# Pool and dense layer of a two-layer trunk: norm rows spread by products, first units in plain fp32, the dense norm put off, and dense steps of 512 columns

## The reference, cut to what matters

```python
for i in range(DEPTH):
    h = rms_norm(x, norm_g[i, 0])
    y = pool_mixer(h, ...) if i == 0 else forgetting_attention(h, ...)
    x = x + rms_norm(y, norm_g[i, 1])
    h = rms_norm(x, norm_g[i, 2])
    y = swiglu(h, ...) if i == 0 else moe_swiglu(h, ...)
    x = x + rms_norm(y, norm_g[i, 3])
```

## Time and profile before

| | |
|---|---|
| median of three runs | 1280.48 us (1279.67 to 1280.71) |
| the profiled execution | 1283.84 us, of which the span is 1281.9 us |
| PE busy | 1224.0 us (95%) |
| DVE, ACT busy | 698.7 us, 542.9 us |
| bytes read | 412.52 MB, 323 GB/s over the span |
| start of the dense layer's second gate unit | 56.69 us |
| end of the dense layer on PE | 238.45 us |
| start of the first pair of heads | 278.58 us |
| last product of the attention's output | 381.24 us |

### The profile page before, as it was taken

One profiled execution on the slowest core, in us unless ns is written; L12 is line 12 of the kernel. 1 busy time (PEld: TensorE's weight loads), 2 busy tenths in 40 slices (PEclk: granted clock), 3 DMA queues, 4 the chain that ended last, 5 costly groups with the idle time before them and its releaser, 6 DMA issues.

```text
span 1281.9 us, 17304 instructions
## 1 busy us (share of the span) xinstructions
PE 1224.0 (95%) x6616; PEld 886.0 (69%) x6616; DVE 698.7 (55%) x781; ACT 542.9 (42%) x516; POOL 105.3 (8%) x119
## 2 busy tenths in 40 slices
PE   8899999889999999999899999989999989999996
PEld 8799999778878788633588853468883347888332
DVE  5754544656657889400598920078871026887102
ACT  4434343355535677300577710067760025775001
POOL 0000000000001222010005001000501000050100
PEclk9899999999999999999999999999999998999999
DMA  9955656453336899999999999999999999999995
GB/s 301 321 195 168 195 166 195 127 165 104 129 120 235 326 373 366 337 401 402 409 409 404 407 409 409 402 409 409 402 409 409 403 407 409 409 402 381 399 402 216
DMA packets 151065, 414.67 MB, mean 323 GB/s; under 512 B 8704, under 2 KB 48640, under 8 KB 150912
## 3 DMA queue, kind: packets, MB, share of 16 engines
q1 hardware_dynamic: 150032, 409.79, 84.6%
q0 software_dynamic: 960, 3.80, 0.9%
HBM read 412.52 MB, written 1.05 MB: 323 GB/s over the span
## 4 chain that ended last, share of the span: by engine, by line
PE 85%; DMA 5%; DVE 4%; issue 2%; SPq 2%; ACT 2%; DVEq 0%; ACTq 0%
PE bank L1229 20%; PE bank L1230 19%; PE bank L1231 19%; PE bank L1516 14%; DMA raw<-in_moe_w_gate 4%; PE bank L1529 4%; SPq L473 1%; PE bank L1469 1%; PE bank L1592 1%; DVE raw_lo L789 1%; PE bank L1546 1%; ACT w_hi L532 1%; DMA raw<-in_pool_w 1%; PE bank L1236 1%; PE bank L1414 1%
## 5 line engine op out<-in xcount | busy, mean ns | idle before, releaser
L789 DVE TENSOR_TENSOR raw_lo<-raw,w_hi 128x2048 fp32r<-128x2048 f32 x170 | 388.4, 2299 | 142.8 <-ACT w_hi L532 142.6
L532 ACT ACTIVATE w_hi<-raw 128x2048 fp32r<-128x2048 f32 x170 | 325.2, 1916 | 225.2 <-PE bank L1231 160.3
L1229 PE MATMUL bank<-w_hi,h_hi 128*128 128x512 f32 (+1 forms) x848 | 301.6, 356 | 30.8 <-DVE h_lo L1084 10.2
L1231 PE MATMUL bank<-w_hi,h_lo 128*128 128x512 f32 (+1 forms) x848 | 296.8, 350 | 0.0
L1230 PE MATMUL bank<-raw_lo,h_hi 128*128 128x512 f32 (+1 forms) x784 | 272.1, 347 | 0.0
L1229 PEld LDWEIGHTS bank<-w_hi,h_hi 128*128 128x128 f32 x848 | 165.0, 195 | 59.9 <-DVE raw_lo L789 22.6
L1231 PEld LDWEIGHTS bank<-w_hi,h_lo 128*128 128x128 f32 x848 | 165.1, 195 | 20.4
L1230 PEld LDWEIGHTS bank<-raw_lo,h_hi 128*128 128x128 f32 x784 | 153.0, 195 | 16.7
L1516 PE MATMUL bank<-raw,h_b 128*64 128x512 f32 (+1 forms) x768 | 143.3, 523 | 0.8 <-DMA raw<-in_moe_w_up 0.7
L1229 PE MATMUL bank<-w_hi,aT_hi 128*128 128x512 f32 x312 | 123.9, 397 | 1.5 <-DVE aT_lo L925 1.5
L1231 PE MATMUL bank<-w_hi,aT_lo 128*128 128x512 f32 x312 | 121.7, 390 | 0.0
(11 more groups left out here) (240 smaller groups left out, 1283.7 us busy)
## 6 DMA issues: line engine op xcount, KB each, us to landing
raw<-in_moe_w_gate SPq DMA_DIRECT2D x96, 1024.0 KB, 15.9
raw<-in_moe_w_up SPq DMA_DIRECT2D x80, 1024.0 KB, 16.1
raw<-in_moe_w_down SPq DMA_DIRECT2D x64, 1024.0 KB, 14.3
raw_extra<-in_moe_w_down SPq DMA_DIRECT2D x48, 1024.0 KB, 16.2
raw_extra<-in_moe_w_up SPq DMA_DIRECT2D x32, 1024.0 KB, 13.5
raw_extra<-in_moe_w_gate SPq DMA_DIRECT2D x16, 1024.0 KB, 14.2
raw<-in_ffn_w_gate SPq DMA_DIRECT2D x11, 1024.0 KB, 5.4
raw<-in_ffn_w_up SPq DMA_DIRECT2D x11, 1024.0 KB, 5.3
```

Source lines behind the costliest of these rows:

```text
L532: nc.scalar.activation(w_hi[:, slot, :], raw_slot(source), ACT.Copy).then_inc(hi_ready, 1)
L789: nc.vector.tensor_tensor(lo_slot(source), raw_slot(source), w_hi[:, slot, :].bitcast(f32), ALU.subtract).then_inc(lo_ready, 1)
L1229: mm(out, a_hi, b_hi, start=first, stop=False)
L1231: return mm(out, a_lo, b_hi, start=False, stop=last)
```

## The change

It touches four places.

First joint. SP loads the three rows (first pre norm, pool scale, first post norm) as single rows of 4 KB, and PE spreads each over the partitions with two products of a row of ones (`row_spread`); DVE's first norm reads its row from PSUM, ACT copies the others to `scale` and `gain`. The pool's product and the first gate and up units (256 columns) take raw weights and a single unsplit activation `h_whole` in plain fp32 (`ffn_first`), so units 0 to 2 are not split. The dense layer's pre norm is put off: x itself is transposed, the channel gain (`gain_t`, loaded as 1024 single floats) is put in as `h_whole` is written, and the token's factor `rstd` goes into the silu and into the product with up. The filler products are 14 instead of 24 at the start, two new lots of 8, and 16 instead of 32 before the transposes.

Dense layer. After the first 256 columns there are five steps of 512: two gate units, two up units and two down units, with the two token blocks in banks of their own, and six slots for the rounded part instead of three. In the last step token block 0 is finished first, and the next joint's transposes for it stand inside the last down unit.

Second joint. `scale_bank(3, 1)` and its chain come after token block 0's `h_lo`. The forget gate's product is made for each token block (128 columns) instead of once for both (256). `head_row` is loaded once `V_U0 + 2` is used.

Third joint. Three parts of the output product, (0, 0), (1, 0) and (0, 1), come ahead of the last heads' transposes.

```diff
-WARM_START = 24
-WARM = (32, 30, 10, 8, 28, 8)
+WARM_START = 14
+WARM = (16, 6, 10, 8, 28, 8, 8, 8)
...
+            for i, row in enumerate((norm_g[0, 0:1, :], pool_scale, norm_g[0, 1:2, :])):
+                sp.dma_start(norm_row[0:1, i, :], row).then_inc(rows_in, 16)
             sp.dma_start(bands[:, :, :], bands_d).then_inc(bands_in, 16)
             load(0, pool_w[0].rearrange("g (b p) n -> p (g b) n", p=P), FG)
-            sp.dma_start(scale[:, :], pool_scale.to_broadcast([P, D])).then_inc(scale_in, 16)
-            sp.dma_start(gain[:, 1, :], norm_g[0, 1:2, :].to_broadcast([P, D])).then_inc(gain_first[1], 16)
             sp.dma_start(consts[:, :], consts_d).then_inc(consts_in, 16)
+            sp.dma_start(gain_t[:, :], norm_g[0, 2, :].rearrange("(k p) -> p k", p=P),
+                         allow_slow_non_contiguous=True).then_inc(gain_t_in, 16)
...
-            hi(0)
-            input_hi(0)
+            row_copy(1, scale, bank[2:4])
+            row_copy(2, gain[:, 1, :], bank[6:8])
+            for b in (0, 2):
+                sc.wait_ge(tr_done, b + 1)
+                nc.scalar.activation(input_part(h_whole, 0, b), bank_blocks(0, b), ACT.Copy).then_inc(whole_act, 1)
             post_squares(1, 0, in_y, (y_done, 2), in_v)
-            hi(1)
+            sc.wait_ge(gain_t_in, 16)
+            whole_act_part(0)
+            post_squares(1, 1, in_y, (y_done, 4), in_v)
             squares(2, 0)
-            post_squares(1, 1, in_y, (y_done, 4), in_v)
-            hi(2)
-            input_hi(1, [0])
+            dense_hi(0)
+            hi(WHOLE_UNITS)
+            whole_act_part(1)
+            dense_hi(1)
             squares(2, 1)
-            input_hi(1, [1])
+            hi(WHOLE_UNITS + 1)
...
+            for s in range(LAST_FS):
+                g = u_gate(s + 1)
+                hi_upto(g + 4)
+                aT_high_dense(s, 0)
+                hi_upto(g + 5)
+                if s > 0:
+                    aT_high_dense(s, 1)
+                for tb in range(TB):
+                    silu_dense(s + 1, tb)
+                hi_upto(g + 7)
...
+            def norm_first(tb):
+                for half in range(2):
+                    cols = slice(half * HALF, (half + 1) * HALF)
+                    nc.vector.scalar_tensor_tensor(xn[:, tb, cols], x[:, tb, cols], rstd[:, 0, tb:tb + 1],
+                                                   bank[4 + half][:, :], ALU.mult, ALU.mult).then_inc(xn_half, 1)
+            def whole_dve_part(tb):
+                ve.wait_ge(tr_done, 4 + 2 * tb + 2)
+                for k in range(4):
+                    step = nc.vector.tensor_scalar(h_whole[:, 4 + k, tb * P:(tb + 1) * P],
+                                                   bank[2 * tb + 1][:, k * P:(k + 1) * P], gain_t[:, 4 + k:5 + k], None,
+                                                   ALU.mult)
+                step.then_inc(whole_dve, 1)
...
-            scale_bank(3, 1, y, ffn_out, None, False)
             root(4, 0)
             norm_x(4, 0)
+            input_lo(2, [0])
+            scale_bank(3, 1, y, ffn_out, (unit_used, V_U0), True)
             root(3, 1)
-            input_lo(2, [0])
             scaled_ready()
             add_normed(3, 1, y)
...
+            def row_spread(i, banks):
+                for half in range(2):
+                    step = mm(banks[half][:, :], silu[0:1, 0:P], norm_row[0:1, i, half * HALF:(half + 1) * HALF],
+                              start=True, stop=True)
+                step.then_inc(rows_psum, 1)
...
+            pe.wait_ge(rows_in, 48)
+            row_spread(0, bank[4:6])
+            row_spread(1, bank[2:4])
+            row_spread(2, bank[6:8])
+            keep_warm(WARM[6], ones)
             pe.wait_ge(bands_in, 16)
-            pe.wait_ge(xn_done, 1)
...
+            pe.wait_ge(rows_done, 2)
+            for k in range(KB):
+                if k % 4 == 0:
+                    pe.wait_ge(xn_half, k // 4 + 1)
                 pool_first(k)
-            pe.wait_ge(xn_done, 2)
-            for k in range(0, KB, 2):
-                pool_second(k)
-                pool_first(k + 1)
-                pool_second(k + 1).then_inc(tr_done, 1)
-            hi, lo = weights(0, FG)
+            pe.wait_ge(rows_done, 4)
+            keep_warm(WARM[7], ones, bank[7])
+            for k in range(KB):
+                if k % 4 == 0:
+                    pe.wait_ge(xn_half, 2 + k // 4 + 1)
+                step = pool_second(k)
+                if k % 2 == 1:
+                    step.then_inc(tr_done, 1)
...
-                        step = three(to, h_hi[:, k, tok], h_lo[:, k, tok], hi[:, k, :], lo[:, k, :], i == 0, i == 1)
+                        step = mm(to, h_whole[:, k, tok], pool_weights[:, k, :], start=(i == 0), stop=(i == 1))
...
+            input_transposed(1, 0)
+            pe.wait_ge(y_done, 4)
+            pe.wait_ge(raw_in[u_gate(0)], landed[u_gate(0)])
+            ffn_first(u_gate(0), bank[4], 0, range(KB))
+            pe.wait_ge(raw_in[u_up(0)], landed[u_up(0)])
+            ffn_first(u_up(0), bank[5], 0, range(4))
+            input_transposed(1, 1)
+            ffn_first(u_up(0), bank[5], 0, range(4, KB))
+            ffn_first(u_gate(0), bank[4], 1, range(KB)).then_inc(unit_used, 1)
+            ffn_first(u_up(0), bank[5], 1, range(KB)).then_inc(unit_used, 1)
+            pe.wait_ge(h_lo_done, h_at(1, 3))
...
+            for s in range(LAST_FS):
+                gate_free = [(silu_done, at_f(s, tb)) for tb in range(TB)] if s > 0 else [None, None]
+                up_free = [(aT_lo_done, at_f(s, tb)) for tb in range(TB)] if s > 0 else [(aT_lo_done, 1), None]
+                ffn_wide(u_gate(s + 1), 0, bank[0:2], gate_free)
+                act_transposed(s, 0)
+                ffn_wide(u_gate(s + 1), 1, bank[0:2], None)
+                if s > 0:
+                    act_transposed(s, 1)
+                for i in range(2):
+                    ffn_wide(u_up(s + 1), i, bank[2:4], up_free)
+                if s < LAST_FS - 1:
+                    pe.wait_ge(aT_lo_done, at_f(s, 1))
+                    for i in range(units_f(s)):
+                        ffn_down(s, i, range(TB))
+            s = LAST_FS - 1
+            pe.wait_ge(aT_lo_done, at_f(s, 1))
+            ffn_down(s, 0, [0])
+            act_transposed(LAST_FS, 0)
+            ffn_down(s, 1, [0]).then_inc(down_half, 1)
+            act_transposed(LAST_FS, 1)
+            pe.wait_ge(aT_lo_done, at_f(LAST_FS, 0))
+            ffn_down(LAST_FS, 0, [0])
+            ffn_down(LAST_FS, 1, [0]).then_inc(y0_psum, 1)
+            ffn_down(s, 0, [1])
+            ffn_down(s, 1, [1])
+            pe.wait_ge(aT_lo_done, at_f(LAST_FS, 1))
+            ffn_down(LAST_FS, 0, [1])
+            ffn_down(LAST_FS, 1, [1], lambda: input_transposed(2, 0))
...
+            pe.wait_ge(small_lo, 2)
+            for tb in range(TB):
+                if tb == 1:
+                    input_transposed(2, 1)
+                pe.wait_ge(h_lo_done, h_at(2, 2 * tb))
                 v_unit(0, [tb])
+                pe.wait_ge(h_lo_done, h_at(2, 2 * tb + 1))
                 v_unit(1, [tb])
-            pe.wait_ge(small_lo, 2)
-            three_t(bank[2][0:H, 0:T], wf2, H).then_inc(f_psum, 1)
-            v_unit(2)
+                step = forget(tb)
+                v_unit(2, [tb])
+            step.then_inc(f_psum, 1)
             v_unit(3)
...
+            pe.wait_ge(o_lo_done, 4)
+            out_part(0, 0)
+            out_part(1, 0)
+            pe.wait_ge(mx_done, H)
+            out_part(0, 1)
+            heads_transposed(H // 2 - 1)
+            head_outputs(H // 2 - 1)
+            out_part(2, 0)
+            out_part(1, 1)
+            pe.wait_ge(o_lo_done, H // 2)
+            out_part(3, 0)
+            out_part(2, 1)
+            out_part(3, 1)
...
+                if n == 4:
+                    po.wait_ge(unit_used, V_U0 + 3)
```

More of the change, by code:

```diff
@@ L156, in sa @@
                 return attn.enter_context(nc.sbuf_tensor(name, shape, dt))
+            with nc.sbuf_tensor("w_hi_q", [P, UNIT], f32r) as w_hi_q:
+                pass
             qk = sa("qk", [P, 2 * T])
@@ L1284, in _ @@
+            pe.wait_ge(raw_in[0], landed[0])
+            pool_weights = part(raw, 0, FG)
             for tb in range(TB):
@@ L1321, in _ @@
[L1321 to L1332 removed]
+            keep_warm(WARM[0], ones)
@@ new lines, in _, with ffn_wide @@
+            pe.wait_ge(h_lo_done, h_at(1, 3))
+            def ffn_wide(u, i, banks, free):
+                hi, lo = weights(u + i, HALF)
+                for tb in range(TB):
+                    tok = slice(tb * P, (tb + 1) * P)
+                    if i == 0 and free[tb]:
+                        pe.wait_ge(*free[tb])
+                    for k in range(4):
+                        kb = 4 * i + k
+                        step = three(banks[tb][:, :], h_hi[:, kb, tok], h_lo[:, kb, tok], hi[:, k, :], lo[:, k, :],
+                                     kb == 0, kb == KB - 1)
```

(12 more changed lines are left out.)

436 lines of the change are left out of this document (264 added, 172 removed).

## The result

| | before | after |
|---|---|---|
| median of six runs each | 1280.6 us | 1276.0 us |
| ratio, 95% interval | | 0.9949 (0.9936 to 0.9962) |
| the profiled execution | 1283.84 us | 1276.08 us |
| its span | 1281.9 us | 1274.2 us |

The kernel is 0.5% faster, by some 6.5 us by the ratio, 4.6 by the two medians and 7.7 by the two profiled spans. The forecast was 1259, with a range of 1253 to 1267: the direction is right, the size is a third of it, and the time lies outside the range.

A forecast was written before the change was run, and what follows sets the result against it. PE, busy 95% of the span, was taken as the bound. Savings of 8.2, 5.1, 5.7 and 2.9 us, passing through the experts whole, sum to 21.9: 1261.9 for the profiled execution, said as 1259 for the median, range 1253 to 1267.

The forecast's parts named there:

- each microsecond ahead of 402 us as a microsecond of the end: At the experts: PE arriving earlier, with all weight slots full, starts the weight stream and ends the kernel equally earlier.
- rival (D): In the experts: their transfers hold the end where it is, 1280 us; chance 0.03.
- First joint: Start to the first 512-column unit: direct transposes of x shorten the chain, unit at 48.5 against 56.69 us; -8.2 us.
- the bounds of K: Price of a one-row `row_spread` product: between 0.907 us, as with 128 rows, and nearly nothing; 0.907 taken.
- Dense layer: Five steps of wide units: 744 products, transposes and last-step waits take 176.7 us against 181.8; -5.1 us.
- b: Price of one 512-column fp32r product, taken as 0.2285 us; 0.2333 would add 4.0 us, 0.2281 save 0.3.
- The wait at the last step: End of the dense layer: 1.0 us kept for waits where the last activation's split follows its transposes.
- Rival (E): Dense steps: up products wait for both transposed activations if a unit lands late; slower, 1284 us at 6.5 us late; chance 0.05.
- Second joint: Dense layer's end to the first heads: 34.4 us against 40.1, with 48 forget-gate products at 0.185 us; -5.7 us.
- the lower bound of 0.114: Forget gate's 128-column products: cheapest price considered, 0.114 us, one record of a filler; 0.185 was taken.
- Rival (B): Forget gate: its narrow products cost 0.114 us, saving 3.4 us more; 1255.4 us, between 1252 and 1256.5; chance 0.25.
- Third joint: Last heads to block 0's result: three output parts fill the softmax wait, 18.9 us against 21.5, plus 0.3 more; -2.9 us.

The follow-up runs named there:

- a1_page: Changed kernel with 28 fillers before the router made 7 of 512 columns, 84 PE instructions fewer ahead of the expert loop; 1263.3 us, ratio 0.9862.
- c_fullrows: Changed kernel with loop and `head_row` wait moved, its six row products given all 128 rows; wrong output, 1468 us, only the start read.

## Why the prediction was wrong, by its own steps

**The step that failed** is "So I count each microsecond ahead of 402 us as a microsecond of the end". It was argued from full slots and from the stream of weights, and a rival (D) was given to the transfers. But the experts' own time was not a constant: the change moved their code on PE, each of its three jumps got a second wait of 2.9 to 3.1 us with a half clock behind it, and the distance from the first gather to the end grew by 11.3 us, which the prediction itself had named as a sign that it fails. Moving the loop alone, either way, makes and takes this: 0.9949 to 0.9862 in the changed kernel, 1 to 1.0068 in the kernel before. With the loop moved and the wait for `head_row` out of the way, the changed kernel takes 1259.4 us, where the forecast was 1259. That the two numbers meet is in part luck, as the next points show; one more piece of it is that this kernel's distance from the gather to the end is 875.8 us, 3.6 less than before. The kernel before has 4.9 us of PE's waits for transfers there, `a1_page` 1.7; why they became fewer is not shown. Rival (D), the end held where it was, falls: with the loop moved and the transfers as they were, the end came earlier.

**First joint**, -8.2 forecast, -4.4 measured. The chain was right, and so was the choice between the bounds of K: at full clock a one-row product takes 2 x 0.43 = 0.86 us, as one with 128 rows does in `c_fullrows` (5.2 us for six), against 0.907 in the sum. What was missing is that the clock falls during such products. With full-height rows the unit starts at 47.59 and 48.27, against 48.5 forecast; the fear that the rows land late did not come true, PE never waited for them.

**Dense layer**, -5.1 forecast, -3.1 measured: the mechanism as told, b mis-sized. The mean spacing of the 512-column products was 0.2305 and not 0.2285, 1.5 us over 744 of them; 0.5 us is left unexplained. The wait at the last step was 1.03 us, as kept. Rival (E) did not occur: no up product waited.

**Second joint**, -5.7 forecast, -9.4 measured, from two errors of opposite sign. The forget gate's products cost 0.06 us and not 0.185, below the lower bound of 0.114, so 48 are 2.9 us: -6.0. The row chosen had 80 rows and another kind of neighbour, and the bound took a filler's record as a floor that it isn't. (Rival (B), which priced them at 0.114, comes to 1258.6 - 3.4 = 1255.2, not 1255.4.) Against it, `head_row`, priced at nothing with 2 us at most, landed 7.87 us after its issue at 253.53, and PE waited 2.8. I had counted to its use and not to the wait, which stands ahead of the whole pair's products.

**Third joint**, -2.9 forecast, -2.1 measured in the changed kernel, 4 us where it was undone. The old order is dearer in the new kernel than it was in its own (97.0 us against 94.5). Its waits are much the same, but the clock was at 0.50 for some 10 us, from 332 to 342, where before it was there for some 3.5; why it came back so much later is left open.

**`gain_t`** cost nothing that a trace shows; its issue took 0.45 us (the row stood on the queue at 4.16), and the units that followed were not missed by PE. The row that the prediction read for it was misread: the same load of `small_w` that held the queue for 4.15 us before was issued in 0.58 us in the changed kernel, and units of 1 MB beside it took 7.08 us before and 4.05 after. The length of such a row is not the price of its short runs.

## What to carry to other kernels

A kernel with a loop in the hardware can pay for where the loop lies in PE's instruction stream (the other engines were not looked at). After any change to the code ahead of it, look behind the jump for a wait that nothing releases in the middle of a run of products, and move the loop by fillers of another width, which leaves PE's work as long as it was. A filler's worth is not PE's busy share: read the granted clock behind every new sort of product. And price a wait where it stands in the program, not where its data is used.

## What the hardware showed that I had not expected

- Behind a taken jump PE issued its first product after a wait of 2.0 to 2.3 us. Where the loop lay badly, the eleventh or twelfth product came 5.4 to 5.7 us after that one, at all twelve such jumps of four profiles, with a wait of 1.26 to 3.10 us ahead of it (DMA at 406 to 418 GB/s at the changed kernel's first). With the loop moved by 36 or 84 instructions there was no such wait. That these are pieces of code being loaded is the reading that fits all of it.
- Six fp32 products of 512 columns with one row of weights, back to back, took the clock from 1.00 to 0.50, PE being busy throughout; with 128 rows the same products left it at 1.00. Two fillers, 0.46 us, between them did not help.
- fp32r products with 16 weight columns came every 0.12 us with 256 moving columns and every 0.06 us with 128: proportional to the columns, with no floor in between.
